# Adding the squares of two neighbouring chunks on VectorE before TensorE sums them

## The reference, cut to what matters

```
def rms_norm_2(x, g):
    y = x32 * lax.rsqrt(jnp.mean(x32 * x32, axis=-1, keepdims=True) + EPS)
    return (y * g)

mix = jnp.concatenate([y_conf, y_att, y_sc, y_pool], axis=-1) @ w_out[i]
h = h + rms_norm_2(mix, g_mix_post[i])
hn = rms_norm_2(h, g_mlp_pre[i])                       # first place
ff = jnp.square(jax.nn.relu(hn @ w_up[i])) @ w_down[i]
h = h + rms_norm_2(ff, g_mlp_post[i])
gate = jax.nn.sigmoid(rms_norm_2(h, g_ple_pre[i]) @ w_ple_gate[i])   # second place
e = (p[i] @ w_ple_proj[i]) * gate
h = h + rms_norm_2(e, g_ple_post[i])
```

## Time and profile before

| what | us |
|---|---|
| median of 3 runs | 2672.24 |
| the profiled execution, its own time | 2673.91 |
| its span | 2672.1 |
| TensorE busy | 2534.1 (95%) |
| VectorE busy | 952.5 (36%) |
| ScalarE busy | 832.8 (31%) |
| GpSimd busy | 859.8 (32%) |

### The profile page before, as it was taken

How to read it: one execution, slowest core, us unless ns; L and a number is a source line. 1 busy time by engine, 2 the same in 40 slices (tenths; PEclk the granted TensorE clock), 3 DMA queues, 4 the chain that set the end, 5 groups by cost and what they waited for, 6 DMA issues and landing times.

```text
span 2672.1 us, 30174 instructions
## 1 busy us (share of the span) xinstructions
PE 2534.1 (95%) x12612; PEld 1968.7 (74%) x12612; DVE 952.5 (36%) x1242; ACT 832.8 (31%) x1233; POOL 859.8 (32%) x414
## 2 busy tenths in 40 slices
PE   7999999999998989999999999989999999999896
PEld 4877778655686656788886667878888888888775
DVE  6323420455204555202278575031122222222423
ACT  4104541455323545313323433232111111112321
POOL 2212212443322112235632212453323333234632
PEclk8999999999998989999999999989999999999897
DMA  7101011100020000013130000201111111111111
GB/s 303 48 24 48 31 34 50 40 20 18 32 76 30 11 21 17 21 59 103 40 110 32 24 25 30 111 24 48 48 48 48 55 48 48 48 48 48 46 40 73
DMA packets 34582, 135.35 MB, mean 51 GB/s; under 512 B 3664, under 2 KB 4112, under 8 KB 33040
## 3 DMA queue, kind: packets, MB, share of 16 engines
q1 hardware_dynamic: 34128, 132.38, 14.3%
q10 hardware_dynamic: 320, 1.05, 0.2%
HBM read 123.97 MB, written 8.39 MB: 50 GB/s over the span
## 4 chain that ended last, share of the span: by engine, by line
PE 84%; DVE 7%; issue 3%; POOL 3%; ACT 2%; DMA 1%; POOLq 0%; ACTq 0%; SPq 0%; DVEq 0%
PE slot L774 54%; PE slot L822 13%; PE ps L1068 2%; PE ps L1044 2%; DVE cacc L2486 2%; PE ps L1029 2%; PE ps L872 1%; POOL wlo L1762 1%; PE ps L1054 1%; PE ps L1122 1%; PE ps L1133 1%; PE ps L1099 1%; PE ps L1111 1%; DVE mm L1966 1%; PE ps L958 1%
## 5 line engine op out<-in xcount | busy, mean ns | idle before, releaser
L774 PE MATMUL slot<-xhi,whi 128*128 128x512 f32 x2192 | 721.1, 408 | 29.2 <-DVE xlo L2552 16.2
L1762 POOL TENSOR_TENSOR wlo<-raw,whi 128x1024 fp32r<-128x1024 f32 (+1 forms) x169 | 434.9, 2573 | 833.6 <-ACT whi L1325 833.6
L774 PE MATMUL slot<-xlo,whi 128*128 128x512 f32 x2192 | 693.3, 396 | 0.0
L774 PE MATMUL slot<-xhi,wlo 128*128 128x512 f32 x2192 | 689.4, 394 | 0.0
L774 PEld LDWEIGHTS slot<-xhi,whi 128*128 128x128 f32 x2192 | 401.8, 191 | 145.1 <-issue 67.9
L774 PEld LDWEIGHTS slot<-xlo,whi 128*128 128x128 f32 x2192 | 419.4, 191 | 91.4
L774 PEld LDWEIGHTS slot<-xhi,wlo 128*128 128x128 f32 x2192 | 417.5, 190 | 91.2
L1325 ACT ACTIVATE whi<-raw 128x1024 fp32r<-128x1024 f32 (+1 forms) x169 | 186.3, 1103 | 304.8 <-PE slot L822 174.4
L1542 ACT ACTIVATE ptr<-ps 128x256 f32<-128x256 f32 (+3 forms) x176 | 80.0, 455 | 276.1 <-PE ps L1044 276.0
L822 PE MATMUL slot<-uhi,whi 128*128 128x512 f32 x512 | 158.3, 390 | 0.0
L822 PE MATMUL slot<-ulo,whi 128*128 128x512 f32 x512 | 157.7, 389 | 0.0
(11 more groups left out here) (346 smaller groups left out, 2847.6 us busy)
## 6 DMA issues: line engine op xcount, KB each, us to landing
raw<-wstream SPq DMA_DIRECT2D x129, 512.0 KB, 3.2
raw<-wstream SPq DMA_DIRECT2D x40, 640.0 KB, 3.9
ada<-wada SPq DMA_DIRECT2D x7, 1024.0 KB, 19.9
mm<-xT SPq DMA_DIRECT2D x2, 2048.0 KB, 9.8
ada<-wada SPq DMA_DIRECT2D x2, 2048.0 KB, 27.5
mm<-xT SPq DMA_DIRECT2D x8, 512.0 KB, 4.1
res_dram<-mm SPq DMA_DIRECT2D x8, 512.0 KB, 3.6
res<-res_dram SPq DMA_DIRECT2D x8, 512.0 KB, 7.2
```

The lines of the kernel that those rows point to most:

```text
L774: o = mm_(outs[:, half * HALF:(half + 1) * HALF], w[b % 2][:, k_w, :], x[:, k_x, half * HALF:(half + 1) * HALF], start=first and j == 0, s ...
L1762: tt(flat(wlo[b % 2])[:, 0:n], (raw1 if b == 1 else raw)[:, 0:n], flat(whi[b % 2])[:, 0:n].bitcast(F32), ALU.subtract).then_inc(w_lo, 1)
```

## The change

Two chunks' squares are added on VectorE (`pair_squares`: chunk n into chunk n's buffer, for n = 1, 3, 5, 7), and TensorE sums the pair: four sums in each stage where there were eight. A new semaphore, `pq_pair`, counts the pairs. ScalarE's squares 3, 5 and 7 now wait for the VectorE add that has read their buffer, and squares 4 and 6 for the sum of the pair. The order of the opening pairs is rewritten: the sums stand behind a3, a5 and a7 and the last one further back.

```
 def opened(events, a, b):
...
-        if i < 4:
+        if i < (5 if a == "u0_0" else 4):
             pair.append(second[i])
-        if a == "u0_0":
-            pair.append(("hsum", 4, i))
-    pair += second[4:]
+        if a == "u0_0" and i in (3, 5, 7):
+            pair.append(("hsum", 4, i - 2))
     if a == "u0_0":
-        pair.insert(-2, ("hrow", 4))
+        pair += second[5:6] + [("hsum", 4, 7)] + second[6:7] + [("hrow", 4)] + second[7:]
+    else:
+        pair += second[4:]
...
 def opened_gates(events):
...
-        if i < 4:
+        if i < 6:
             pair.append(g1[i])
-        pair.append(("hsum", 6, i))
-    pair += g1[4:6] + [("hrow", 6)] + g1[6:8] + g0[8:] + g1[8:]
+        if i in (3, 5, 7):
+            pair.append(("hsum", 6, i - 2))
+    pair += g1[6:7] + [("hsum", 6, 7)] + g1[7:8] + [("hrow", 6)] + g0[8:] + g1[8:]
...
             def chunk_sum(k, j, n):
-                if k and n == 0:
+                if n == 1:
                     pe.wait_ge(nstd, k)
-                pe.wait_ge(pq_done, 8 * j + n + 1)
-                square_sums(0, sring[n % 3], n == 0, n == 7).then_inc(pq_used if n < 7 else nsum, 1)
+                pe.wait_ge(pq_pair, 4 * (j - 1) + n // 2 + 1)
+                square_sums(0, sring[n % 3], n == 1, n == 7).then_inc(pq_used if n < 7 else nsum, 1)
...
             def chunk_square(j, n, src):
                 if n < 3:
                     act.wait_ge(nsum, (0, 4, 6)[j])
+                elif n % 2:
+                    act.wait_ge(pq_pair, 4 * (j - 1) + (n - 3) // 2 + 1)
                 else:
-                    act.wait_ge(pq_used, 7 * (j - 1) + n - 2)
+                    act.wait_ge(pq_used, 3 * (j - 1) + (n - 4) // 2 + 1)
...
+            def pair_squares(k, n):
+                j = 1 if k == 3 else 2
+                dve.wait_ge(pq_done, 8 * j + n + 1)
+                v.tensor_tensor(sring[n % 3][:], sring[n % 3][:], sring[(n - 1) % 3][:], ALU.add).then_inc(pq_pair, 1)
...
+                        if m in (3, 5, 7):
+                            pair_squares(k, m - 2)
+                    pair_squares(k, 7)
                     v.tensor_copy(wide_row, rstd(k + 1)).then_inc(napplied, 1)
```

More of the change, by code:

```diff
@@ L608, in build @@
         pe_order = sem("pe_order")
+        pq_pair = sem("pq_pair")
         kh_done, kl_done, qh_done, ql_done, ada_acc, s_fac = (
```

## The result

The changed kernel takes 2683.47 us (median of 6 runs, 2679.61 to 2689.30) against 2673.03 for the kernel before beside it: ratio 1.0040, 95% interval 1.0024 to 1.0055, **slower by about 10.4 us**. Measured again on another occasion it gave 2681.02 (12 runs), ratio 1.0024 (1.0013 to 1.0034), 6.4 us slower. The forecast of 2676.1 had the sign, and its +3.9 us is 37% of the first measurement and 61% of the second; its range ended at 2682.

A forecast was written before the change was run, and what follows sets the result against it. TensorE was taken as the bound, its 15.2 us saved returning as waits for chunks: 1.6 at full clock + 1.5 + 0.8 for clock falls = +3.9 on 2672.24, giving 2676.1 us; range 2668 to 2682.

The forecast's parts named there:

- The loop: Both stages: add, square, high part, low part wait in turn, so TensorE waits some 2 us for chunk 4 and again later.
- the gain of 7.6 a stage: TensorE, each stage: four sums of 1.90 us removed, 7.6 us, 15.2 in both, the most that can be gained.
- rival D: TensorE keeps the gain because squares and high parts don't wait for adds: stages 5.6 and 4.7 us earlier, 2662 us; chance 0.09.
- The adds: VectorE, each stage: first two adds near 3.3 us beside GpSimd's residual adds, last two about 1.25 with GpSimd idle.
- rival C: The adds are cheap: the first two cost 2.2 us each instead of 3.3, giving 2671.7 us; chance 0.14.
- Low part 7 at 19.2 behind low part 3: Both stages: chunk 7's low part ends 19.2 us behind chunk 3's, where it was 14.8 in the first stage.
- the term of 0.8 for the clock: Both stages: half clock before a4 is mostly hidden by TensorE's wait for pair 3; 0.8 us added for all such falls.
- The tail and the broadcast: Second stage, behind the last low part: 9.5 us of TensorE work, then 2.84 of uncovered waiting for the slot before `yhi`.
- The half clock behind the pause: Second stage: the 2.84 us wait behind the broadcast brings half clock for the `yhi` parts, costing 1.5 us.
- The sum: Whole kernel: 1.6 us at the full clock (0.4 first stage, 1.2 second) plus 1.5 and 0.8 for the clock, +3.9.
- Rival B: The clock keeps falling, decisive behind the last low part: two to four more losses, 2679 to 2682, say 2680.6; chance 0.27.

The follow-up runs named there:

- noadds: The changed kernel with eight square buffers and without each stage's four adds, even squares left out of the norm: 2665.42 us, ratio 0.9963 to the kernel before.
- mid8: The changed kernel with eight square buffers, adds behind GpSimd's last residual add, one part held back ahead of the broadcast and two behind: 2667.83 us, ratio 0.9976.
- s3_first: The changed kernel with the sum of chunks 2 and 3 moved ahead of part b5 in stage 2: 2677.70 us, ratio 1.0022 to the kernel before.
- stage2_only: The kernel before with pair adds and four sums in the second stage only: 2684.24 us, ratio 1.0049.
- fill4: The changed kernel with ten unread matmuls ahead of part g0 4 in stage 2: 2676.35 us, ratio 1.0013 to the kernel before.
- fill: The changed kernel with ten unread matmuls ahead of each of parts g0 4, 7 and 8 in stage 2: 2676.29 us, ratio 1.0007 to the kernel before.

## Why the prediction was wrong

- **The loop, right.** Squares waited for VectorE, TensorE for low parts 4 and 7, and the gain of 7.6 a stage was gone. noadds and mid8 agree that rival D needed another arrangement.
- **The adds, right.** 3.4 us for add 1 and add 3 (3.3 forecast), 1.22 for add 5 and add 7 (1.25). The 2.2 of rival C didn't appear: the adds beside GpSimd took 3.38 to 3.42 in every profile, and 1.21 behind its last add in mid8. The Trainium skill (SBUF — State Buffer, Who interferes with whom) has the rule that a VectorE instruction with two SBUF inputs contends with a GpSimd instruction that reads SBUF, for the ports that they share, one at a time. These times agree.
- **Low part 7 at 19.2 behind low part 3: right for stage 1 as long as the clock's fall was short (19.25, and 19.97 in the other profile), wrong for stage 2 (21.77). This is the step that failed**, and with it the term of 0.8 for the clock. It has two halves. "Second stage: ... with the same 19.2" carried the first stage over, though the change puts b5 ahead of sum 3 in the second stage and not in the first. And "a fall before a4 is mostly hidden, since TensorE waits for pair 3 anyway" held only for a short fall and a TensorE with no more to do before sum 3 than in stage 1. The stretches that the prediction showed at the half clock were 3.4 us long; this one lasted 6.8. So a4, b4, a5 and b5 took until 2.5 us behind add 3, and the loop handed that on through square 6 and high part 7. The forecast had 0.8 for all such falls; this one was worth 2.57. The table under s3_first shows it in five steps.
- **The tail and the broadcast, right.** From low part 7 to `yhi` 9.5 + 2.84 + 0.1 = 12.44 was forecast and 2557.23 - 2544.81 = 12.42 came. The half clock behind the pause cost 1.60 (9.78 from `yhi` to `g` against 8.18), forecast 1.5.
- **The sum.** Stage 1 cost 1.10 and 0.41 in two profiles (0.4 forecast without the clock), stage 2 5.36 (2.7 without the 0.8). Together 5.8 to 6.5, against 3.9 forecast. That agrees with the second measurement, 6.4 (3.5 to 9.1), and reaches only the lower end of the first (6.4 to 14.7). Where the first one's other 4 us are is open, though the two measurements themselves overlap. The profile of stage2_only shows one way, a single execution that lost 10.8 us up to `yhi`, 7.1 more than the change's profiles; how often that happens in timed runs was not seen.
- **Rival B** came nearest in size (2680.6), with the half clock as its cause. Its condition, a fall behind the last low part, is met in stage2_only, not in the two profiles of the whole change, where the costly fall lay before low part 7.

## What to carry to other kernels

Work taken off the busiest engine is only a gain if the engine that takes it over doesn't stand in the loop that feeds the first one: ask which buffer the new operation holds, and put it behind the last producer, with buffers enough to wait there, as mid8 does. When a schedule is worked out for one stage, work it out again for the other one in its own order of instructions. A clock fall is hidden only while what it delays has slack: compare the time at which the delayed sum would run with the time its input is ready.

## What the runs showed of the hardware

- A pause of 2.4 to 2.9 us on TensorE was often followed by a half clock, and not always. In the second stage of the change the clock was at a half for 6.8 us around the end of the pause of 2.77 ahead of a4 and for 3.4 us behind the 2.77 ahead of `yhi`, and stayed at full behind the 2.43 ahead of a7. Ahead of `yhi` it also stayed at full in fill4, with the same pause of 2.77.
- The same place of the same program had half clocks of different lengths: 6.7 and 3.4 us in the first stage of the change's two profiles. Such a doubling was worth 0.7 us there. What decides the length is not shown.
- The clock also fell without a pause just before: in mid8 from 2531.3 to 2538.1, in the third one-column sum in a row, 9 us behind the last pause, although TensorE was busy all the time between.
- Matmuls that nobody reads went with a full clock where they fitted into the pause (ahead of a4 in fill4 and fill; the other twelve stages of the table had a half clock there), and cost time where the clock was at a half already (fill: ten of them took 3.10 us ahead of a7, against 2.14 ahead of a4).
- The same kernel twice, and 11.6 us between the spans (2683.9 and 2672.3) with the second stage alike to 0.01 us: at this size of effect the difference of two profiles says nothing until it is taken inside the stage.
